# The beginning of a two-block transformer kernel on one core: input transfers, constant products and bias products in another order

## The reference

```python
def first_block(x, rel_table, attn_norm, ffn_norm, final_norm, a_w_qkv, a_b_qkv, a_sinks, a_w_o, a_b_o,
              b_w_in, b_cmp_pos, b_cmp_w1, b_cmp_w2, b_w_o, ffn_w_gu, ffn_w_down):
    h = x
    for layer in range(DEPTH):
        hn = rms_norm(h, attn_norm[layer])
        ...
            h = h + swa_sink_mixer(hn, a_w_qkv[j], a_b_qkv[j], a_sinks[j], a_w_o[j], a_b_o[j], rel_table)
        ...
        h = h + swiglu(rms_norm(h, ffn_norm[layer]), ffn_w_gu[layer], ffn_w_down[layer])
    return rms_norm(h, final_norm)

def rms_norm(x, g):
    x32 = x.astype(jnp.float32)
    y = x32 * lax.rsqrt(jnp.mean(x32 * x32, axis=-1, keepdims=True) + RMS_EPS)
    return (y * g.astype(jnp.float32)).astype(x.dtype)

def swa_sink_mixer(h, w_qkv, b_qkv, sinks, w_o, b_o, rel_table):
    ...
    qkv = h @ w_qkv + b_qkv
    q = qkv[..., :ATTN_WIDTH].reshape(B, S, A_KV_HEADS, g_sz, HEAD_DIM) * HEAD_DIM ** -0.5
    ...
    o = banded_attention(q, k, v, A_WINDOW, rel_table, sinks)
    return o.reshape(B, S, ATTN_WIDTH) @ w_o + b_o

def banded_attention(q, k, v, window, rel_table, sinks):
    ...
    bias = head_bias(rel_table, dist, hkv)
    ...
        s = jnp.einsum('bqhgd,bshd->bhgqs', qn, kn).astype(jnp.float32) + bias
    ...
```

## Time and profile before

| | us |
|---|---|
| median of 3 runs | 1988.1 |
| lowest and highest run | 1982.8, 1988.7 |
| the profiled execution | 1986.4 |
| its span in the trace | 1984.7 |

### The profile page before, as it was taken

The page is one execution under the profiler, slowest core; times in us unless marked ns, Lnnn a source line. Parts: engine busy times, 40 slices in busy tenths (PEclk is TensorE's granted clock), DMA queues, the critical chain, the costliest instruction groups (busy, mean ns, idle before and its releaser), DMA issues.

```text
span 1984.7 us, 29527 instructions
## 1 busy us (share of the span) xinstructions
PE 1932.2 (97%) x9826; PEld 1625.8 (82%) x9826; DVE 1056.7 (53%) x2323; ACT 831.5 (42%) x1528; POOL 792.5 (40%) x392
## 2 busy tenths in 40 slices
PE   7999999999999999999999999999999999999997
PEld 5897888888878899888888888888788888777886
DVE  5464655321274777546653444666614666565645
ACT  4464322222344777543222223422222356666622
POOL 3533454444444211145444443444544333324441
PEclk9999999999999999999999999999999999999999
DMA  7532545333225112125453222323223221212121
GB/s 239 168 105 98 189 167 181 109 99 98 96 92 155 38 48 67 48 97 200 165 184 106 96 95 85 107 96 99 98 95 99 71 85 54 74 51 76 64 86 43
DMA packets 70020, 209.52 MB, mean 106 GB/s; under 512 B 9739, under 2 KB 15115, under 8 KB 69948
## 3 DMA queue, kind: packets, MB, share of 16 engines
q1 hardware_dynamic: 57724, 174.72, 26.9%
q10 hardware_dynamic: 12224, 33.85, 5.2%
HBM read 196.90 MB, written 8.49 MB: 103 GB/s over the span
## 4 chain that ended last, share of the span: by engine, by line
PE 83%; DVE 8%; ACT 2%; issue 2%; POOL 1%; DVEq 0%; ACTq 0%; POOLq 0%
PE bank L1026 21%; PE bank L1028 21%; PE bank L1027 21%; PE bank L1394 3%; PE bank L1591 2%; PE bank L1343 2%; PE bank L1374 1%; PE bank L1446 1%; PE bank L1244 1%; PE bank L1572 1%; PE bank L1583 1%; DVE rstd L1669 1%; PE bank L1451 1%; PE bank L1232 1%; PE bank L1221 1%
## 5 line engine op out<-in xcount | busy, mean ns | idle before, releaser
L471 POOL TENSOR_TENSOR wsp<-raw,wsp 128x1024 fp32r<-128x1024 f32 (+2 forms) x291 | 705.4, 2429 | 947.6 <-ACT wsp L581 942.6
L1026 PE MATMUL bank<-xs,wsp 128*128 128x512 f32 x1304 | 513.6, 394 | 4.3 <-DVE mid L2199 1.7
L581 ACT ACTIVATE wsp<-raw 128x1024 fp32r<-128x1024 f32 (+2 forms) x294 | 302.6, 1037 | 508.8 <-PE bank L1028 466.7
L1028 PE MATMUL bank<-xs,wsp 128*128 128x512 f32 x1304 | 508.7, 390 | 0.0
L1027 PE MATMUL bank<-xs,wsp 128*128 128x512 f32 x1304 | 508.5, 390 | 0.0
L1026 PEld LDWEIGHTS bank<-xs,wsp 128*128 128x128 f32 x1304 | 245.5, 188 | 57.0 <-issue 7.4
L1028 PEld LDWEIGHTS bank<-xs,wsp 128*128 128x128 f32 x1304 | 245.3, 188 | 51.9
L1027 PEld LDWEIGHTS bank<-xs,wsp 128*128 128x128 f32 x1304 | 245.5, 188 | 50.5 <-issue 1.0
L1026 PE MATMUL bank<-gsp,wsp 128*128 128x512 f32 x512 | 200.1, 391 | 2.2 <-issue 1.2
L1028 PE MATMUL bank<-gsp,wsp 128*128 128x512 f32 x512 | 199.3, 389 | 0.0
L1027 PE MATMUL bank<-gsp,wsp 128*128 128x512 f32 x512 | 199.2, 389 | 0.0
(11 more groups left out here) (322 smaller groups left out, 2773.1 us busy)
## 6 DMA issues: line engine op xcount, KB each, us to landing
raw<-weights SPq DMA_DIRECT2D x294, 512.0 KB, 3.5
gen<-ada ACTq DMA_DIRECT2D x48, 512.0 KB, 3.5
tmp<-mid SPq DMA_DIRECT2D x64, 128.0 KB, 3.0
bias_b<-bias_row ACTq DMA_DIRECT2D x1, 4096.0 KB, 36.9
mid<-bias_b SPq DMA_DIRECT2D x8, 512.0 KB, 4.1
hT<-xT SPq DMA_DIRECT2D x2, 1024.0 KB, 9.6
bias_a<-bias_row ACTq DMA_DIRECT2D x1, 2048.0 KB, 16.9
mid<-bias_a SPq DMA_DIRECT2D x8, 256.0 KB, 3.1
```

What stands on the lines that cost most here:

```text
L471: pool.tensor_tensor(wsp[:, slot, 1, 0:w], raw[:, slot, 0:w], wsp[:, slot, 0, 0:w].bitcast(F32), ALU.subtract).then_inc(w_ready, 1)
L581: act.activation(wsp[:, u % RING, 0, 0:w], raw[:, u % RING, 0:w], ACT.Copy).then_inc(hi_done, 1)
L1026: pe.matmul(dst, w[0], x[0], start=first, stop=False)
L1028: return pe.matmul(dst, w[1], x[0], start=False, stop=last)
```

## The change

The work is the same; 30 filler matmuls are added and the rest is ordered anew.

- SP issues unit 0, both halves of the input and unit 1 first, then `rel`, `onehot` and `rows` (which leaves ACT's queue), then units 2 and 3.
- PE starts with `keep_running(bank[7], 30)`. Then come the key and value products, the mean, and only then the four bias products, in banks 2, 4, 5 and 6 in place of 1 to 4. The wait for ACT's copy of them stands before the second query product; it stood before the value product.
- DVE makes the low halves of units 0 and 1; POOL starts with unit 2.
- ACT loads its table of functions while the first weights are under way, does the squares right after unit 2 is split, splits unit 3 behind the last square (before the root), then takes the root, splits unit 4, copies and stores the bias row, and issues the two big bias transfers only behind the split of unit 6.
- DVE waits for the bias products before it writes the keys, as both use `gen`.

The diff, cut to its core:

```diff
...
-            sp.wait_ge(consts, 1)
-            sp.dma_start(gen[0:32, 0:HEADS], rel).then_inc(rel_in, 16)
-            sp.dma_start(gen[0:33, 16:16 + BIAS_COLS], onehot).then_inc(rel_in, 16)
...
             def load(slot, unit):
                 sp.dma_start(raw[:, slot, :], weights[unit]).then_inc(raw_in[slot], 16)
...
+            load_one(0)
             for n in range(2):
-                load_one(n)
                 sp.dma_start(hT[:, 4 * n:4 * n + 4, :],
                              xT.rearrange("(j p) t -> p j t", p=P)[:, 4 * n:4 * n + 4, :]).then_inc(x_in[n], 16)
+            load_one(1)
+            sp.wait_ge(consts, 1)
+            sp.dma_start(gen[0:32, 0:HEADS], rel).then_inc(rel_in, 16)
+            sp.dma_start(gen[0:33, 16:16 + BIAS_COLS], onehot).then_inc(rel_in, 16)
+            sp.dma_start(rowp[:, :], rows.partition_broadcast(P)).then_inc(rows_in, 16)
             load_units(2, A_O + RING)
             sp.wait_ge(bias_stored, 48)
...
-            split_units(0, A_O + AHEAD)
+            pool.wait_ge(w_ready, 2)
+            for u in range(2, RING):
+                split_lo(u, u)
+            split_units(RING, A_O + AHEAD)
...
             act.dma_start(colp[:, :], cols).then_inc(cols_in, 16)
-            act.dma_start(rowp[:, :], rows.partition_broadcast(P)).then_inc(rows_in, 16)
+            act.wait_ge(consts, 6)
+            act.activation(credit[:, 11:12], eps[:, 0:1], ACT.Copy)
+
+            split_hi(0)
             act.wait_ge(cols_in, 16)
-            act.wait_ge(consts, 6)
-
-            split_hi(0)
             scaled_hi("attn0", 0)
             for u in range(1, AHEAD):
                 split_hi(u)
-
+            squares(0, (A_K + AHEAD,))
+            split_hi(A_V + AHEAD)
             brow = gen[0:HEADS, 2048:2048 + BIAS_COLS]
             act.wait_ge(brow_mm, 4)
             for n in range(4):
                 w = BIAS_COLS // 4
-                act.activation(brow[:, w * n:w * n + w], bank[1 + n][0:HEADS, 0:w], ACT.Copy).then_inc(brow_copied, 1)
+                act.activation(brow[:, w * n:w * n + w], bank[BIAS_BANKS[n]][0:HEADS, 0:w], ACT.Copy).then_inc(brow_copied, 1)
             act.wait_ge(brow_copied, 4)
             act.dma_start(bias_row, brow).then_inc(bias_stored, 16)
-            squares(0)
-            act.wait_ge(bias_stored, 16)
-            act.dma_start(bias_a, bass.AP(bias_row.tensor, 127, [[BIAS_COLS, HEADS], [-1, P], [1, 256]])
-                          ).then_inc(bias_stored, 16)
-            act.dma_start(bias_b, bass.AP(bias_row.tensor, 384 + 127, [[BIAS_COLS, HEADS], [-1, P], [1, 512]])
-                          ).then_inc(bias_stored, 16)
-            split_hi(A_K + AHEAD)
-            split_hi(A_V + AHEAD)
             act.wait_ge(k_raw, 1)
             act.activation(a_ks[0:HD], a_k, ACT.Copy).then_inc(k_hi, 1)
-            with act.Fori(0, 2) as i:
-                for k in range(RING):
-                    split_hi(A_Q + k + AHEAD, i)
+            for u in range(A_Q + AHEAD, A_Q + DC + AHEAD):
+                split_hi(u)
+                if u == A_Q + AHEAD + 1:
+                    act.wait_ge(bias_stored, 16)
+                    act.dma_start(bias_a, bass.AP(bias_row.tensor, 127, [[BIAS_COLS, HEADS], [-1, P], [1, 256]])
+                                  ).then_inc(bias_stored, 16)
+                    act.dma_start(bias_b, bass.AP(bias_row.tensor, 384 + 127, [[BIAS_COLS, HEADS], [-1, P], [1, 512]])
+                                  ).then_inc(bias_stored, 16)
 
...
+            pe.wait_ge(consts, 6)
+            keep_running(bank[7], 30)
+            project(A_K, bank[0][:, :], norm=0)
+            project(A_V, bank[1][:, :])
+            mean_square(0)
             pe.wait_ge(rel_in, 32)
             for n in range(4):
                 w = BIAS_COLS // 4
-                pe.matmul(bank[1 + n][0:HEADS, 0:w], gen[0:33, 0:HEADS], gen[0:33, 16 + w * n:16 + w * n + w],
+                pe.matmul(bank[BIAS_BANKS[n]][0:HEADS, 0:w], gen[0:33, 0:HEADS], gen[0:33, 16 + w * n:16 + w * n + w],
                           start=True, stop=True).then_inc(brow_mm, 1)
-            pe.wait_ge(consts, 6)
-            project(A_K, bank[0][:, :], norm=0)
-            pe.wait_ge(brow_copied, 4)
-            project(A_V, bank[1][:, :])
-            mean_square(0)
             for i in range(2):
                 if i:
                     pe.wait_ge(v_feat, 1)
                     to_tokens(bank[1], a_vf).then_inc(v_mm, 1)
                 for k in range(RING):
                     pe.wait_ge(q_free, i * RING + k + 1)
+                    if not i and k == 1:
+                        pe.wait_ge(brow_copied, 4)
                     u = A_Q + i * RING + k
                     half = project(u, bank[3 + k][:, :], part=range(4))
...
             def split_lo(u):
 
                 dve.wait_ge(hi_done, u + 1)
-                dve.wait_ge(w_ready, u)
+                if u:
+                    dve.wait_ge(w_ready, u)
                 dve.tensor_tensor(wsp[:, u % RING, 1, :], raw[:, u % RING, :], wsp[:, u % RING, 0, :].bitcast(F32),
                                   ALU.subtract).then_inc(w_ready, 1)
 
...
+            split_lo(0)
             dve.wait_ge(cols_in, 16)
             scaled_lo(0, "attn0")
+            split_lo(1)
             dve.wait_ge(rows_in, 16)
             step(dve.tensor_scalar(bq8[:, :], colp[:, COL["bq"]:COL["bq"] + DC], HD ** -0.5, None, ALU.mult))
             rms(0)
             dve.wait_ge(unit_used, A_K + 1)
             step(dve.tensor_tensor(tmp[:, 0, :], bank[0][:, :], rstd[:, :], ALU.mult))
+            dve.wait_ge(brow_mm, 4)
             for g in range(KV):
                 x = dve.tensor_scalar(a_k[:, g, :], tmp[g * HD:g * HD + HD, 0, :], col("bk")[g * HD:g * HD + HD], None,
                                       ALU.add)
```

More of the change, by code:

```diff
@@ L62 @@
 UNITS = O_O + 16
+BIAS_BANKS = (2, 4, 5, 6)
 SHARED = (B_W1 + 4, B_W1 + 6, B_Q)
@@ L581, in split_hi, with scaled_hi @@
                 act.activation(wsp[:, u % RING, 0, 0:w], raw[:, u % RING, 0:w], ACT.Copy).then_inc(hi_done, 1)
-            def scaled_hi(gain, base):
-                for j in range(DC):
+            def scaled_hi(gain, base, tiles=range(DC)):
+                for j in tiles:
                     if base:
```

## The result

The changed kernel takes **1996.16 us** (median; 1990.89 to 2005.05) against 1984.15 (1981.81 to 1988.69) for the kernel before in the same comparison: ratio 1.0062, 95% interval 1.0042 to 1.0083. The forecast was 1991.0, the range ended at 1996.0, and "within 0.3%" had the largest chance; it is slower by 0.6%. A second comparison of the same file gave 1.0070 (1.0054 to 1.0087). The profiled execution of after took 1990.89, the quickest of its seven, so its trace holds less than the whole loss.

The account below looks back on a forecast made before the run. PE, busy 97% of the span, bounds the kernel. Query products +3.5 and bias chain up to 0.5 make +4 on the profiled 1986.4, 1990.4; allowing for that execution lying below the median, forecast 1991 us, range 1983.5 to 1996.

Parts of the forecast that it names:

- Squares at 16.3: ACT before the mean: squares follow unit 2's split at once and begin at 16.3, 4.6 us earlier.
- Filler ends 11.2, products at 22.1: PE's start: filler raises the clock and ends at 11.2; key and value products end at 22.1.
- Collision 2.1, sums end 26.3: POOL's split of unit 3 falls on DVE's last two additions, adding 2.1 us; sums end at 26.3.
- PE idle 4.2: Before the mean: PE waits 4.2 us for DVE's sums, instead of 1.3.
- The clock falls there: After the idle gap, at mean and bias products, PE falls to half rate; forecast case's chance 0.45.
- It costs 4.0 over the full-rate sum, and PE is 3.5 later: Full-rate sum starts first query product at 29.6; half rate adds 4.0, leaving PE 3.5 later from the second.
- `bias_a` at 40.3, `bias_b` takes 3 us less than its 36.9 after units 7 to 9 are out of its way, lands 71.0: Bias chain before attention: late issue, partly paid back, lands `bias_b` at 71.0, bounds 68 to 74.
- the slow end: End of `bias_b`'s transfer, with few DMA engines working, may shrink: 0 to 6 us allowed, 3 taken.
- Attention 3.5 to 4 later: Start of attention: PE's delay and the bias chain, within a microsecond of each other, make it 3.5 to 4 later.
- the bias table is what attention waits for: Rival: `bias_b` again takes 36.9 us, attention starts 7 to 10 later; 1994 to 1998 us, chance 0.13.
- After the start of attention the program is as before, so the shift is carried to the end.: From attention onward: nothing new arises, so the beginning's shift, +4 us, reaches the end unchanged.
- the forecast's doubt about products with so few rows and columns of weights: Bias products, 33 rows and 16 columns of weights, ran from 6.28 to 11.95 without the clock rising.

Follow-up runs that it names:

- a_own: Changed kernel with `bias_b` counted on another semaphore, so SP's query copies no longer wait for it; 1997.56 us, ratio 1.0077.
- a_again: The changed kernel measured once more, without edits; 1996.25 us, ratio 1.0070.
- a_pad24: Changed kernel with twenty-four one-column VectorE memsets ahead of its first low half; 1989.33 us, ratio 1.0032.
- a_fill_own: Changed kernel with 20 filler matmuls between value products and mean, and `bias_b` on its own count; 1989.99 us, ratio 1.0036.
- b_pad2: Kernel before the change with two one-column VectorE memsets added near the start; 1982.55 us, ratio 1.0002.
- b_pad4: Kernel before the change with four one-column VectorE memsets added near the start; 1991.42 us, ratio 1.0037.
- best1: Changed kernel: bias products then three constant passes before mean, bias row and transfers early, unit 3 split behind root, own `bias_b` count, sixteen memsets; 1988.97 us.
- best2: best1 with twenty-four VectorE memsets in place of sixteen; 1978.43 us, ratio 0.9977.
- a_fill_own_pad24: a_fill_own with twenty-four one-column VectorE memsets added; 1982.98 us, ratio 1.0001.
- a_fill: Changed kernel with 20 more filler matmuls between the value products and the mean; 1990.41 us, ratio 1.0042.

## Why the prediction was wrong

Point by point.

- *Squares at 16.3*: 16.61. *Filler ends 11.2, products at 22.1*: the filler ends at 11.16, the products at 22.1. *Collision 2.1, sums end 26.3*: 2.2, and 26.78; of the 0.5, 0.3 is the later start of the squares. *PE idle 4.2*: 4.76. Right, each within 0.6. (The first half of the input came at 8.55 and not near 7, and SP started 0.1 earlier and not 0.3; the filler ran until 11.16, so neither held PE up.)
- *The clock falls there*: it did. *It costs 4.0 over the full-rate sum, and PE is 3.5 later*: 5.2. **This term was too small.** The sum kept the mean at 0.55, and at half rate it took from 26.83 to 28.76; the sums' end was 0.5 late.
- *`bias_a` at 40.3, `bias_b` takes 3 us less than its 36.9 after units 7 to 9 are out of its way, lands 71.0*: issued at 41.53 and 42.22, 32.4 to land, so 74.6. For a start 10.9 later the forecast allowed 6.9 us of gain (3.9 for the units, 3 for the slow end); the start was 12.2 later, and 4.5 came. The landing lies outside the bounds of 68 to 74. *Attention 3.5 to 4 later*: 6.9 in the profiled execution. The rival "the bias table is what attention waits for" did occur (a query split at 79.05, foreseen at 79.5 to 82.5). The time too lies in its band of 1994 to 1998, but that is luck: the rival had all of the loss at the start of attention, and about half of it, by the medians, arose in the loop. What this wait costs by itself was not measured: a_own, which takes it away, was no faster, with the 2.2 us that it won lost again in the loop.
- *After the start of attention the program is as before, so the shift is carried to the end.* **This is the step that failed.** The change adds four instructions to VectorE's program ahead of a loop of 280 which could move by two places and not by four, and the loop then waits twice at its branch, 3.8 us each. Its price, as the difference of the ratios, each against before in its own set: 7.5 us by a_again and a_pad24, 6.9 by the pair a_fill_own, 6.9 by b_pad2 and b_pad4, 10.9 by best1 and best2 (by the bare medians 6.9, 7.0, 8.9 and 10.5).

In medians: the beginning costs 6.9 (a_pad24 over before), and filling the gap and giving `bias_b` its own count take away nearly all of that together (a_fill_own_pad24 over before: 0.5). With the loop's waits present the filling alone gave 5.8 and the count alone nothing; how the 6.9 is shared without the waits is open. The loop costs about as much again, 7 us. That the two add up to a_again's 14.7 over before says little, as the loop's price is taken from the same kernel; what confirms it is the pair b_pad2 and b_pad4, which has nothing of the change in it. The forecast had 4 of all this. It also started near 1987, from three executions and the profiled one, where the seven of the comparison gave 1984.15 and later sets 1981.4 to 1982.5. So the true shift in that comparison was 12.0, the forecast 8.0 short of it, and the starting point, 2.9 too high, hid a third of the error.

What stays open: whether the clock falls behind a wait. In the changed kernel it did in a_again's profiled execution and not in the first one's, with the same 3.8 us waits. Its executions ranged over 14 us, and their mean granted clocks from 0.985 to 0.994 go with that; best2's, without gap or waits, range over 2 us at 0.996 to 0.998. I have not shown what decides it in a single execution. Nor is it shown what made it fall behind the bias products in a_fill_own_pad24, where PE had not been idle; the forecast's doubt about products with so few rows and columns of weights is not settled by a_fill alone. Nor was the collision of POOL and DVE (2.2 us on the sums) undone alone; best2, which avoids it and the gap together, has its six additions in 4.68.

The idea of the change itself was sound: with the bias products in the gap instead of behind it, the bias transfers early, and the loop placed well, it gives 0.23% (best2: the second query product at 32.35, 3.7 earlier than before).

```profile
21.73 2.94 PE L1204 MATMUL bank<-gen 33*16 33x412 f32 x8
24.60 0.94 PE L1088 MATMUL bank<-ident,mean_w 128*128 128x128 f32 x6
25.38 1.02 PE L1109 MATMUL bank<-rstd,mean_w 128*128 128x512 f32 x2
...
32.35 0.47 PE L1033 MATMUL bank<-xs,wsp 128*128 128x512 f32 x1 [0.48 <-POOL wsp L474]
```

## What to carry to other kernels

Count the instructions of every engine ahead of its loops, before and after an edit, with those that only wait: a loop of 280 VectorE instructions was tipped over by four added instructions 650 us ahead of it, and the sign is a wait on "issue" at the loop's first instruction together with more packets on the instruction queue. Work that moves off an engine's critical path should be put into an idle gap, not behind it: here the clock that the filler had raised was gone after 4.76 us of idle, and everything behind the gap, short products too, is priced at half rate. Where a visible wait (here for the bias table) ends last, remove it alone before believing its price, and if the time stays, follow the lead through the trace: here it was won and lost again in the loop.

## What was not expected of the hardware

- A VectorE loop of 280 instructions runs without waits (q14 28 or 29 packets) when it lies 0, 1, 2 or 28 places on, and with a wait at its branch (38 or 39 packets) at 4 and 20. The wait is 3.8 us, or 2.7 and 1.9 in two parts. That it is a fetch of instructions is inferred from the queue's packets and from the place. The packets are 8 KB each (28 for 0.23 MB). The bad stretch begins at 3 or 4 and ends between 20 and 28. This agrees with the 23 places estimated above from the block of 256 instructions in the Trainium skill, Runtime: NRT & Kernel Launch, section Instruction fetch mechanics; a count from the packet had failed.
- A stop of one engine of 3.8 us that left PE idle for only 0.9 was followed in b_pad4 by a granted clock of 0.50 to 0.53 for about 10 us (720 to 730). PE's other short idles in the same loop, 0.8 each, left it at 1.00, and so did the same wait in the changed kernel's profiled execution.
- The wait is worth 1.6 us per pass with the clock up and about 5 with it down, so where the clock falls it is the larger part of the price.
